# Three projected query tiles between the attention's first scores, and an opening that scales tokens from PSUM

## The chip, the cores and the metric

The kernel runs on 1 core of one Trainium2 chip (trn2). The metric is the device time of one execution in microseconds (us); lower is better.

## The reference

A two-layer encoder trunk is applied to two sequences (`x_prompt` and `x_sample`, 512 tokens of 1,024 numbers each), which share one set of weights. 16 learned meta tokens stand before every sequence and are dropped from the output. All is float32.

- Every layer computes h = h + Mixer(RMSNorm(h)) and then h = h + SwiGLU(RMSNorm(h)).
- Layer 0's mixer is multi-head latent attention (4 heads) beside a short gated convolution; both read one projection of the normalised input, by `mla_w_in`.
- Layer 1's mixer is grouped-query attention: `qkv = h @ w_qkv`, 8 query heads and 2 key/value heads of 128 columns. Queries and keys are RMS-normalised for each head, multiplied by a gain and rotated by two-dimensional positions:

```
q = rms_norm(q, q_g); k = rms_norm(k, k_g)
q = concat(rotate(q[..., :64], ang_rows), rotate(q[..., 64:], ang_cols))   # k likewise
o = softmax(q k^T / sqrt(128)) v
rotate(x1, x2) = (x1 cos - x2 sin, x2 cos + x1 sin)
```

## The kernel before

**Products.** Each float32 operand is held as a high part, rounded to the matmul's format (`_hi`), and the residue (`_lo`). A product is three matmuls, low x high, high x low and high x high (`product`, L164 to L166). The high part is rounded on ScalarE (ACT), the residue is subtracted on VectorE (DVE) or, for weights, on GpSimd (POOL).

**Order of work.** There is no planner. Each engine's instructions are written out by hand as a loop; the phases pass hooks to one another (`then`, `vector_at`, `gpsimd_at`, `items_at`), and engines wait for semaphore counts. Each engine and each DMA queue works its list strictly in order.

**Opening (`gates_steps`).** Eight token tiles of 128 x 1,024 (`x_rows`) and weight units of 128 x 1,024 are loaded by SyncE (SP), meta tokens and small gains by ScalarE's queue. For each tile TensorE transposes 8 blocks into two PSUM banks (`turn_tile`, L485), ScalarE copies them to `h` (`copy_tile`, L368), VectorE multiplies `h` by the norm's gain into `xg` (`scale_tile`, L565), ScalarE rounds (`round_tile`, L374), VectorE subtracts (`split_tile`, L571). ScalarE also rounds the weight units (`round_unit`, L361), GpSimd splits them (L462), and ScalarE squares the rows for the norm (L380). `group(q)` multiplies one weight unit with 352 token columns, 24 matmuls; 36 groups follow one another. The first needs 3 tiles and meta (`ready_for`). Transposition of all 49 rows of gains (L524) waits for all seven small DMAs. TensorE's order is: tile 0, gains, meta, tiles 1 to 5, group 0, tiles 6 and 7, groups 1 to 4, the first scale rows, group 5.

**Layer 1's projections (`qkv_steps`).** `work` has 25 tiles of 128 tokens x 512 columns: 9 of keys and values, then 8 and 8 of queries; numbers 17 to 24 are the last 8 (heads 4 to 7). A tile is 24 matmuls of 512 columns on TensorE, then on ScalarE four squares with a row sum and one copy (`L1267`, `L1273`), on GpSimd a multiplication by the gain (L1288), on VectorE the rotation (`rotate`, `rope_heads`, L661 to L666: six operations on 128 x 256). The last tile is rotated by GpSimd within the attention (`rotate_last`, L1382 to L1390, at tiles 3, 4 and 6). `invert_last` finds the inverse norms of the last 8 tiles on VectorE in five parts, at tiles 3 to 7.

```
banks = [n % 6 for n in range(ends[1])] + [6, 7, 0, 1, 2, 3, 6, 7]     # L1173
if 3 <= n < 8: invert_last(dve, link, n - 3)                            # L1407
if n in (3, 4, 6): rotate_last(pool, (3, 4, 6).index(n))                # L1411
```

**Layer 1's attention (`attention_steps`).** 16 units (sequence, head) of 4 query tiles make 64 tiles n; the keys are new in every fourth unit. For tile n: TensorE makes the scores (two halves, three matmuls each; banks 0 to 3 in turn), VectorE the row maximum (`maximum`, L2072), ScalarE the exponentials (L1898), VectorE the reciprocal of their sum (`invert`, L2079), GpSimd the normalisation and a repeat of the meta columns (L1831, L1835), TensorE transposes the probabilities (`turn_probs`, L1993, L1999, from step n + 2), ScalarE rounds them (L1874), VectorE subtracts (L2049), TensorE multiplies with the values (`output`). GpSimd stages the queries and keys of the unit after next (L1796, L1769) at the second to fourth tile of a unit; TensorE transposes them (L1961). VectorE's step n is: reciprocal of tile n - 1, maximum of n, hook `vector_at`, the finished output's residue, staged items, residues of tile n - 2.

Of the kernel before, what the change touches and what calls it, by code (L numbers as in the profile page):

```python
# [93 lines left out]
def program(nc, x_prompt, x_sample, meta_tokens, mix_norm_g, ffn_norm_g, mla_w_in, mla_q_a_g, mla_kv_a_g,  # L94
# [3 lines left out]
    with ctx:  # L98
# [153 lines left out]
        def gates_steps():  # L252
# [7 lines left out]
            const_in, gains_in, x_in = sem("const_in"), sem("gains_in"), [sem(f"x_in{i}") for i in range(9)]  # L260
            made, turned, gains_t, gains_ready = sem("made"), sem("turned"), sem("gains_t"), sem("gains_ready")
# [37 lines left out]

            def seqs(a, lo, hi):  # L300
                return a.rearrange("p (s t) -> p s t", s=SEQS)[:, :, lo:hi]
# [7 lines left out]
            def sync(sp, load_piece):  # L309
# [38 lines left out]
            def scalar(act, round_piece):  # L348
                act.dma_start(meta_rows, meta_tokens).then_inc(x_in[8], 16)
                for n, (src, l) in enumerate(((mix_norm_g, 0), (ffn_norm_g, 0), (mix_norm_g, 1), (ffn_norm_g, 1))):  # L350
                    act.dma_start(g_rows[KC * n:KC * (n + 1), :],
                                  src[l].rearrange("(c p) -> c p", p=P)).then_inc(gains_in, 16)
# [10 lines left out]
                def copy_tile(i):  # L363

                    act.wait_ge(turned, place(i))
                    t0 = tile_column(i)
                    b = 4 + 2 * (i % 2)
                    A.activation(h[:, :, t0:t0 + P], PS[:, b:b + 2, :].rearrange("p b (c t) -> p (b c) t", c=4),  # L368
                                 ACT.Copy).then_inc(h_copied, 1)
# [12 lines left out]
                def copy_meta():  # L382
                    act.wait_ge(turned, 2)
                    for s in range(SEQS):
                        last = A.activation(h[:, :, s * LEN:s * LEN + META],
                                            PS[:, 3, 0:KC * META].rearrange("p (c t) -> p c t", c=KC), ACT.Copy)
# [92 lines left out]
            def tensor(pe):  # L479
# [23 lines left out]
                def group(q):  # L503
# [10 lines left out]
                    if n < START:  # L514
                        pe.wait_ge(x_split, ready_for[g])
                    for k in range(KC):
# [6 lines left out]
                pe.wait_ge(gains_in, 16 * 7)  # L523
                T.transpose(PS[:, 2, 0:49], g_rows, ident[0:49, 0:49]).then_inc(gains_t, 1)  # L524
# [18 lines left out]
            def vector(dve):  # L543
# [15 lines left out]
                def scale_tile(i):  # L559

                    dve.wait_ge(h_copied, place(i))
                    t0 = tile_column(i)
# [27 lines left out]
                def drain(q):  # L590
# [8 lines left out]
                V.tensor_copy(gain_cols[:, :], PS[:, 2, 0:49]).then_inc(gains_ready, 1)  # L599
                dve.wait_ge(gains_ready, 1)  # L600
                scale_tile(0)
                dve.wait_ge(h_copied, 2)
                V.tensor_tensor(meta_xg, h[:, :, 0:META], gain.unsqueeze(2).broadcast_to([P, KC, META]),
                                ALU.mult).then_inc(x_scaled, 1)
                split_tile(0)
                scale_tile(1)
# [5 lines left out]
                for i in range(2, 8):  # L612
                    scale_tile(i)
                    split_tile(i - 1)
                find_rstd(0)
                split_tile(7)
# [537 lines left out]
        def qkv_steps():  # L1154
# [18 lines left out]
            banks = [n % 6 for n in range(ends[1])] + [6, 7, 0, 1, 2, 3, 6, 7]  # L1173
# [53 lines left out]
            def sync(sp):  # L1227
# [8 lines left out]
                at = work[last][1] % TILES * P  # L1236
# [1682 lines left out]
```

## Time and profile before

| What | us |
|---|---|
| median of 3 runs (lowest to highest) | 2351.49 (2349.76 to 2353.48) |
| the profiled execution, its own time | 2351.51 |
| its span (first to last instruction) | 2349.7 |
| TensorE busy | 2286.0 |
| VectorE, GpSimd, ScalarE busy | 1254.6, 1245.1, 900.0 |

The profile is of one execution. "Span" runs from the first instruction to the last. PE is TensorE's matmuls, PEld its weight loads, DVE VectorE, ACT ScalarE, POOL GpSimd, SP SyncE; a q behind a name is an engine's DMA queue. L12 is line 12 of the kernel. A matmul's duration overlaps that of the next, so the distance of starts is its price; so it is with VectorE's and ScalarE's operations, to a lesser degree. "Idle before" is the time in which the engine had nothing to run before an instruction, with what ended it. PEclk is the granted clock of TensorE as a share of its full 2.4 GHz.

### The profile page before, as it was taken

The numbers are of one execution on the slowest core, as the hardware profiler recorded it, in microseconds if no ns is written. First come the engines' busy times: TensorE is split into PE (matmuls) and PEld (weight loads), VectorE is DVE, ScalarE is ACT, GpSimd is POOL, SyncE is SP. The second block draws the span as 40 slices with busy tenths as digits, with TensorE's granted clock in tenths as the row PEclk, the third lists the DMA queues.
The fourth block names the chain that finished last, engine by engine and source line by source line (L and its number), as shares of the span: only waits on it lengthen the run. The fifth ranks groups of instructions, "written<-read, shape, count | busy, mean of one in ns | idle before, by whom it ended". The sixth has DMA issues, their size and how long they took to land.

```text
span 2349.7 us, 37598 instructions
## 1 busy us (share of the span) xinstructions
PE 2286.0 (97%) x14574; PEld 2084.4 (89%) x14574; DVE 1254.6 (53%) x2017; ACT 900.0 (38%) x1893; POOL 1245.1 (53%) x1048
## 2 busy tenths in 40 slices
PE   7999989999999999999999998999999999999998
PEld 7999878999999999999998778988878888888887
DVE  5221467459444444444449568855954444444444
ACT  5125666445222222222225446754532222222222
POOL 1344388545455555555543347764555555555561
PEclk9999999999999999999999999999999999999999
DMA  5131001432111111111112000023211111111112
GB/s 207 46 107 64 23 20 41 161 86 72 50 50 46 55 55 55 50 50 46 43 48 76 28 3 2 2 84 92 72 54 53 51 54 52 49 53 51 54 54 76
DMA packets 187505, 137.26 MB, mean 58 GB/s; under 512 B 7361, under 2 KB 176210, under 8 KB 187330
## 3 DMA queue, kind: packets, MB, share of 16 engines
q1 hardware_dynamic: 187200, 134.77, 18.7%
q8 instruction: 118, 1.93, 0.3%
q14 instruction: 57, 0.47, 0.1%
q10 hardware_dynamic: 130, 0.09, 0.0%
HBM read 121.69 MB, written 12.85 MB: 57 GB/s over the span
## 4 chain that ended last, share of the span: by engine, by line
PE 81%; DVE 10%; issue 4%; ACT 3%; POOL 2%; DMA 0%; ACTq 0%; DVEq 0%; POOLq 0%
PE PS L164 26%; PE PS L166 26%; PE PS L165 26%; PE PS L1993 1%; DVE stat L2072 1%; DVE w_lo L2049 1%; DVE b_lo L2693 1%; PE PS L1961 1%; DVE x_raw L2689 1%; DVE x_hi L2720 0%; DVE x_lo L216 0%; DVE t L2713 0%; POOL w_lo L462 0%; ACT w_hi L1874 0%; DVE t L2711 0%
## 5 line engine op out<-in xcount | busy, mean ns | idle before, releaser
L2387 POOL TENSOR_TENSOR w_lo<-stage,w_hi 128x512 fp32r<-128x512 f32 x374 | 506.4, 1358 | 613.7 <-ACT w_hi L2383 611.5
L2383 ACT ACTIVATE w_hi<-stage 128x512 fp32r<-128x512 f32 x374 | 233.2, 628 | 558.5 <-PE PS L166 558.4
L2786 DVE TENSOR_TENSOR hT<-hT,PS 128x528 f32<-128x528 f32 (+1 forms) x384 | 266.6, 695 | 309.4 <-PE PS L166 308.7
L164 PE MATMUL PS<-x_hi,w_lo 128*128 128x264 f32 (+2 forms) x1092 | 352.8, 323 | 8.2 <-DVE x_lo L571 5.1
L164 PE MATMUL PS<-s_hi,w_lo 128*128 128x264 f32 (+1 forms) x1104 | 354.4, 321 | 4.1 <-DVE s_lo L2732 3.1
L166 PE MATMUL PS<-s_hi,w_hi 128*128 128x264 f32 (+1 forms) x1104 | 353.9, 321 | 0.0
L165 PE MATMUL PS<-s_lo,w_hi 128*128 128x264 f32 (+1 forms) x1104 | 352.6, 319 | 0.0
L166 PE MATMUL PS<-x_hi,w_hi 128*128 128x264 f32 (+2 forms) x1092 | 351.7, 322 | 0.0
L165 PE MATMUL PS<-x_lo,w_hi 128*128 128x264 f32 (+2 forms) x1092 | 351.1, 322 | 0.0
L164 PE MATMUL PS<-b_hi,w_lo 128*128 128x264 f32 (+1 forms) x864 | 278.4, 322 | 1.4 <-DVE a L2796 1.4
L165 PE MATMUL PS<-b_lo,w_hi 128*128 128x264 f32 (+1 forms) x864 | 277.5, 321 | 0.0
L166 PE MATMUL PS<-b_hi,w_hi 128*128 128x264 f32 (+1 forms) x864 | 276.8, 320 | 0.0
L164 PEld LDWEIGHTS PS<-x_hi,w_lo 128*128 128x128 f32 x1092 | 206.4, 189 | 20.8 <-issue 5.3
L164 PEld LDWEIGHTS PS<-s_hi,w_lo 128*128 128x128 f32 x1104 | 207.6, 188 | 19.4 <-issue 4.8
L166 PEld LDWEIGHTS PS<-s_hi,w_hi 128*128 128x128 f32 x1104 | 207.8, 188 | 15.9
L165 PEld LDWEIGHTS PS<-s_lo,w_hi 128*128 128x128 f32 x1104 | 207.3, 188 | 16.3
L166 PEld LDWEIGHTS PS<-x_hi,w_hi 128*128 128x128 f32 x1092 | 206.6, 189 | 11.6
L165 PEld LDWEIGHTS PS<-x_lo,w_hi 128*128 128x128 f32 x1092 | 206.1, 189 | 11.8
L164 PEld LDWEIGHTS PS<-b_hi,w_lo 128*128 128x128 f32 x864 | 162.5, 188 | 16.9 <-issue 4.5
L166 PEld LDWEIGHTS PS<-b_hi,w_hi 128*128 128x128 f32 x864 | 162.6, 188 | 12.6
L165 PEld LDWEIGHTS PS<-b_lo,w_hi 128*128 128x128 f32 x864 | 162.5, 188 | 12.2
L164 PE MATMUL PS<-x_lo,w_lo 128*128 128x264 f32 (+1 forms) x480 | 154.1, 321 | 3.4 <-issue 2.1
(373 smaller groups left out, 4917.5 us busy)
## 6 DMA issues: line engine op xcount, KB each, us to landing
stage<-in_ffn_w SPq DMA_DIRECT2D x280, 256.0 KB, 2.8
stage<-in_even_w_out SPq DMA_DIRECT2D x32, 256.0 KB, 2.7
stage<-in_odd_w_out SPq DMA_DIRECT2D x32, 256.0 KB, 2.7
stage<-in_mla_w_in SPq DMA_DIRECT2D x12, 512.0 KB, 6.5
stage<-in_gqa_w_qkv SPq DMA_DIRECT2D x12, 512.0 KB, 3.7
h_spill<-hT SPq DMA_DIRECT2D x8, 528.0 KB, 5.1
hT<-h_spill SPq DMA_DIRECT2D x8, 528.0 KB, 6.7
conv_hi<-s_hi SPq DMA_DIRECT2D x4, 528.0 KB, 2.7
```

The lines of the kernel that those rows point to most:

```text
L164: T.matmul(out, a_lo, b_hi, start=first, stop=False)
L165: T.matmul(out, a_hi, b_lo, start=False, stop=False)
L166: return T.matmul(out, a_hi, b_hi, start=False, stop=last)
L1961: last = T.transpose(PS[:, bank, j * P:(j + 1) * P], k_stage[:, staged_main(s, j), c * P:(c + 1) * P] if kind == "k" else q_stage[:, stage ...
L1993: T.transpose(PS[:, 4 + turn[("p", n, 0)] % 2, c * P:c * P + m], p[0:m, c * P:(c + 1) * P], ident[0:m, 0:m])
L2049: V.tensor_tensor(lo, src, hi.bitcast(F32), ALU.subtract).then_inc(lo_ready, 1)
L2072: V.tensor_reduce(shifts[0:rows, b:b + 1], PS[0:rows, 2 * (n % 2):2 * (n % 2) + 2, 0:HALF], mybir.AxisListType.XY, ALU.min).then_inc(shift, 1)
L2383: A.activation(ring(w_hi, n), source(n), ACT.Copy).then_inc(rounded, 1)
L2387: G.tensor_tensor(ring(w_lo, n), source(n), ring(w_hi, n).bitcast(F32), ALU.subtract).then_inc(split, 1)
L2689: V.tensor_tensor(x_of(c, s), x_of(c, s), tt_row, ALU.mult).then_inc(xhat, 1)
L2693: V.tensor_tensor(bl(c // 4, s, c % 4), x_of(c, s), bh(c // 4, s, c % 4).bitcast(F32), ALU.subtract).then_inc(x_split, 1)
L2786: V.tensor_tensor(o, o, sums(st.slot), ALU.add).then_inc(drained, 1)
```

## The change

Two parts.

**Opening.** VectorE scales tokens from the transposition's PSUM banks instead of `h`; it no longer waits for ScalarE's copy, and the copy now waits for the scaling. Gains are transposed and copied in two goes, the first norm's 8 columns first, with a semaphore of their own; all 49 rows again after tile 1. SyncE loads the first weight unit before tile 2 (before: after it); ScalarE's queue issues the first gain before meta. ScalarE starts with rounding the first unit and then, for each tile, rounds before it copies. TensorE multiplies group 0 after tile 3, group 1 after tile 5.

**Layer 1.** Only 22 tiles are projected before the attention; tile 22 is multiplied after scores 1, tiles 23 and 24 after scores 2 (`tensor_at`), evicted by ScalarE at steps 1, 2 and 3 (`scalar_at`). The last four tiles (21 to 24) are scaled by GpSimd at tiles 8, 12, 16 and 20 and rotated by VectorE in three parts each, at tiles 12 to 14, 16 to 18, 20 to 22 and 24 to 26, with tables loaded anew. `invert_last` moves to tiles 5 to 9. Exponentials of tile 2 are put before the rounding of staged items.

```diff
-                for i in range(3):
+                for i in range(2):
                     load_x(i)
                 load_unit(0)
-                load_x(3)
+                for i in range(2, 4):
+                    load_x(i)
...
                 def copy_tile(i):
-                    act.wait_ge(turned, place(i))
+                    act.wait_ge(x_scaled, place(i))
...
+                round_unit(0)
+                round_tile(0)
+                round_meta()
                 copy_tile(0)
                 copy_meta()
-                round_tile(0)
+                round_tile(1)
                 copy_tile(1)
-                round_meta()
                 for i in range(2, 8):
+                    round_tile(i)
                     copy_tile(i)
-                    round_tile(i - 1)
-                    if i in (2, 3, 4):
-                        round_unit(i - 2)
-                    if i == 4:
+                    if i in (2, 3):
+                        round_unit(i - 1)
+                    if i == 3:
                         square_meta(0)
-                    if i >= 4:
-                        square_rows(i - 4)
-                round_tile(7)
+                    if 3 <= i < 7:
+                        square_rows(i - 3)
...
-                for i in range(1, 6):
+                turn_tile(1)
+                pe.wait_ge(gains_in, 16 * 6)
+                pe.wait_ge(gains_ready, 1)
+                T.transpose(PS[:, 2, 0:49], g_rows, ident[0:49, 0:49]).then_inc(gains_t, 1)
+                for i in range(2, 4):
                     turn_tile(i)
                 group(0)
+                for i in range(4, 6):
+                    turn_tile(i)
+                group(1)
                 for i in (6, 7):
                     turn_tile(i)
-                for q in range(1, 5):
+                for q in range(2, 5):
                     group(q)
...
-                    dve.wait_ge(h_copied, place(i))
+                    dve.wait_ge(turned, place(i))
                     if i >= 2:
                         dve.wait_ge(x_split, place(i - 2))
-                    V.tensor_tensor(xg[i % 2], h[:, :, t0:t0 + P], gain.unsqueeze(2).broadcast_to([P, KC, P]),
+                    V.tensor_tensor(xg[i % 2], turned_tile(i), gain.unsqueeze(2).broadcast_to([P, KC, P]),
...
+                scale_tile(2)
+                split_tile(1)
+                split_tile(2)
+                dve.wait_ge(gains_t, 2)
+                V.tensor_copy(gain_cols[:, KC:49], PS[:, 2, KC:49]).then_inc(gains_ready, 1)
+                scale_tile(3)
+                for i in range(4, 8):
                     scale_tile(i)
                     split_tile(i - 1)
...
-            banks = [n % 6 for n in range(ends[1])] + [6, 7, 0, 1, 2, 3, 6, 7]
+            roped_late, filling = len(work) - 4, len(work) - 3
+            banks = [n % 6 for n in range(ends[1])] + [6, 7, 2, 3, 6, 7, 6, 7]
...
+            def sync_late(sp):
+                sp.wait_ge(last_roped, 1)
+                load_late_table(sp, last)
...
             def vector_at(dve, link, n):
-                if 3 <= n < 8:
-                    invert_last(dve, link, n - 3)
+                if 5 <= n < 10:
+                    invert_last(dve, link, n - 5)
+                unit, j = divmod(n - 12, MAIN)
+                if 0 <= unit < 4 and j < 3:
+                    rotate_late(dve, roped_late + unit, j)
 
             def gpsimd_at(pool, n):
-                if n in (3, 4, 6):
-                    rotate_last(pool, (3, 4, 6).index(n))
+                if n in (8, 12, 16, 20):
+                    scale_tile(pool, roped_late + n // 4 - 2)
+
+            def tensor_at(pe, n):
+                if n == 0:
+                    multiply(pe, filling)
+                if n == 1:
+                    multiply(pe, filling + 1)
+                    multiply(pe, filling + 2)
+
+            def scalar_at(act, n):
+                if n in (1, 2, 3):
+                    evict(act, filling + n - 1)
...
             def wait_scores(pe, n):
                 if n == 0:
-                    pe.wait_ge(copied, len(work) - 2)
+                    pe.wait_ge(copied, ends[1])
+                if n == 1:
+                    pe.wait_ge(copied, roped_late)
...
-                    if not L0 and n == first_steps.queries_after + 5:
+                    if not L0 and n == first_steps.queries_after + 3:
                         stage_heads(1)
...
+                            if not L0:
+                                first_steps.wait_weights(act)
                             round_values(0)
```

`rotate_late` makes the same six operations on VectorE as `rotate_last` made on GpSimd, two for each part: two products, two products, a difference and a sum; both inputs of each lie in SBUF. `multiply` and `evict` are the bodies of the former loops. `wait_weights` waits for the last projected tile, since the values' high part overwrites the weights. The probabilities' first transposition waits for the eviction of tile 23, the first output for that of tile 24.

## Rows read from the trace of the kernel before

**Rows 1.** the page, busy time of each engine: us (share of the span), instructions.

```profile
PE 2286.0 (97%) x14574; PEld 2084.4 (89%) x14574; DVE 1254.6 (53%) x2017; ACT 900.0 (38%) x1893; POOL 1245.1 (53%) x1048
```

**Rows 2.** timeline, opening, TensorE: start, us, engine, line, what, [idle before <- released by].

```profile
5.48 1.94 PE L485 MATMUL PS<-ident,wide 128*128 128x128 f32 x8 [5.48 <-DMA wide<-in_x_prompt]
...
23.38 0.63 PE L164 MATMUL PS<-x_hi,w_lo 128*128 128x352 f32 x1 [5.13 <-DVE x_lo L571]
...
29.23 1.91 PE L485 MATMUL PS<-ident,wide 128*128 128x128 f32 x16
```

**Rows 3.** timeline, opening: ScalarE, VectorE and GpSimd.

```profile
8.89 1.23 DVE L565 TENSOR_TENSOR mid<-hT,gain_cols 128x1024 f32<-128x1024 f32 x1
...
14.14 1.05 ACT L374 ACTIVATE x_hi<-mid 128x1024 fp32r<-128x1024 f32 x1
...
16.22 2.65 POOL L462 TENSOR_TENSOR w_lo<-stage,w_hi 128x1024 fp32r<-128x1024 f32 x1 [14.65 <-ACT w_hi L361]
...
17.08 2.87 DVE L565 TENSOR_TENSOR mid<-hT,gain_cols 128x1024 f32<-128x1024 f32 x1 [0.44 <-ACT hT L368]
...
19.87 3.37 DVE L571 TENSOR_TENSOR x_lo<-mid,x_hi 128x1024 fp32r<-128x1024 f32 x1
```

**Rows 4.** timelines, end of layer 1's projections and start of its attention: ScalarE, TensorE.

```profile
1383.97 0.37 ACT L1267 ACTIVATE wide<-PS,stat 128x128 f32<-128x128 f32 x1 [3.93 <-PE PS L166]
...
1400.67 0.37 ACT L1267 ACTIVATE wide<-PS,stat 128x128 f32<-128x128 f32 x1 [1.82 <-PE PS L166]
...
1403.63 0.39 PE L164 MATMUL PS<-s_hi,s_lo 128*128 128x264 f32 x1 [1.52 <-ACT tmp L1898]
...
1405.30 0.66 PE L1993 MATMUL PS<-ident,tmp 128*128 128x128 f32 x4 [0.23 <-POOL tmp L1831]
...
1419.81 0.63 PE L1993 MATMUL PS<-ident,rope 128*128 128x128 f32 x4 [1.25 <-DVE s_lo L2049]
```

**Rows 5.** timeline, layer 1's attention, TensorE, the same place of two neighbouring units.

```profile
1445.26 0.65 PE L1993 MATMUL PS<-ident,tmp 128*128 128x128 f32 x4 [0.22 <-POOL tmp L1831]
...
1454.34 0.66 PE L1993 MATMUL PS<-ident,gain_rows 128*128 128x128 f32 x4 [0.20 <-POOL gain_rows L1831]
```

**Rows 6.** windows, a unit and one with new keys: PE, PEld, DVE, ACT, POOL.

```profile
1453.01:1462.09 9.08, 8.88 (x76) 8.67 (x75) 7.89 (x16) 6.83 (x17) 6.53 (x10) 1.00 0.01 2
1433.93:1445.03 11.10, 9.84 (x79) 8.97 (x77) 8.54 (x19) 7.60 (x20) 6.58 (x11) 1.00 0.00 0
```

**Rows 7.** sources, opening: weight load issued at 2.1, third token tile at 1.7.

```profile
DMA to landing us min/median/max: 7.1/7.1/7.1
...
DMA to landing us min/median/max: 6.2/6.2/6.2
```

**Rows 8.** windows, opening: busy of five engines, granted clock, DMA share, GB/s.

```profile
23.00:24.00 1.00, 0.62 (x2) 0.65 (x3) 0.90 (x2) 0.97 (x2) 1.00 (x1) 0.50 0.42 70
```

**Rows 9.** timeline, opening, VectorE: the drain of a later group.

```profile
61.25 0.52 DVE L594 TENSOR_TENSOR wide<-PS,mid 128x352 f32<-128x352 f32 x1 [3.34 <-PE PS L166]
```

**Rows 10.** timeline, layer 1's attention, VectorE: reciprocal of one tile, maximum of the next.

```profile
1453.01 0.16 DVE L2079 RECIPROCAL stat<-stat 128x1 f32<-128x1 f32 x1
1453.20 0.71 DVE L2072 TENSOR_REDUCE stat<-PS 128x1 f32<-128x528 f32 x1
```

**Rows 11.** timeline, layer 1's attention, GpSimd: normalisation and repeat of a tile.

```profile
1455.25 1.04 POOL L1831 TENSOR_TENSOR rope<-rope,stat 128x512 f32<-128x512 f32 x1
1456.25 0.35 POOL L1835 TENSOR_TENSOR tmp<-rope,stat 128x96 f32<-128x96 f32 x1
```

**Rows 12.** timelines, VectorE and GpSimd: two-operand operations in SBUF side by side.

```profile
1324.82 2.60 DVE L661 TENSOR_TENSOR tmp<-wide,rope 128x256 f32<-128x256 f32 x1 [3.35 <-POOL wide L1288]
...
1324.73 2.40 POOL L1225 TENSOR_TENSOR w_lo<-stage,w_hi 128x1024 fp32r<-128x1024 f32 x1
...
1414.60 0.97 DVE L188 SCALAR_TENSOR_TENSOR stat<-stat,tmp 128x32 f32<-128x32 f32 x1
```

**Rows 13.** groups by form, 1420 to 1560: count | busy, mean ns | idle.

```profile
L2049 DVE TENSOR_TENSOR w_lo<-PS,w_hi 128x512 fp32r<-128x512 f32 x59 | 40.6, 688 | 12.0 <-ACT w_hi L1874 11.9
```

More of the change, by code:

```diff
@@ L1283, in gpsimd @@
                 pool.wait_ge(consts, 48)
-                for n, (b, i) in enumerate(work):
-                    heads = heads_of(n)
-                    pool.wait_ge(copied, n + 1)
-                    o = place(n).rearrange("p (h n) -> p h n", h=heads)
-                    G.tensor_tensor(o, o, gains[b == 2].unsqueeze(1).broadcast_to([P, heads, HD]),
-                                    ALU.mult).then_inc(scaled, 1)
+                for n in range(roped_late):
+                    scale_tile(pool, n)
                     if n in piece_after:
@@ L1292, in gpsimd, with multiply @@
                     then(n)
+            def multiply(pe, n):
+                b, i = work[n]
+                t0 = token_column(i)
+                block_ = sum(n >= e for e in ends)
+                earlier = [m for m in range(n) if banks[m] == banks[n]]
+                if earlier:
+                    pe.wait_ge(copied, earlier[-1] + 1)
+                else:
+                    steps.wait_bank(pe, banks[n])
+                if banks[n] == 7 and not earlier:
+                    pe.wait_ge(norm.rstd_ready, 2)
+                if i == MAIN:
+                    pe.wait_ge(gathered, 2)
+                for k in range(KC):
+                    if n == 0 or n in ends:
+                        pe.wait_ge(split, 4 * block_ + k // 2 + 1)
+                    if n < ONCE:
+                        norm.wait_x(pe, 1 - i // TILES, k)
+                    out = PS[0:meta_cols, banks[n], :] if i == MAIN else PS[:, banks[n], :]
+                    hi, lo = (metas[part][:, k, :] if i == MAIN else (x_hi, x_lo)[part][:, k, t0:t0 + P] for part in range(2))
+                    product_ = product(out, hi, lo,
+                                       weights(block_, 0, k), weights(block_, 1, k), k == 0, k == KC - 1)
+                product_.then_inc(done, 1)
             def tensor(pe, then):
-                for n, (b, i) in enumerate(work):
-                    t0 = token_column(i)
+                for n in range(filling):
                     if n == 1:
@@ L1300, in tensor @@
                         norm.average(pe, 1)
-                    block_ = sum(n >= e for e in ends)
-                    earlier = [m for m in range(n) if banks[m] == banks[n]]
-                    if earlier:
-                        pe.wait_ge(copied, earlier[-1] + 1)
-                    else:
-                        steps.wait_bank(pe, banks[n])
-                    if banks[n] == 7 and not earlier:
-                        pe.wait_ge(norm.rstd_ready, 2)
-                    if i == MAIN:
-                        pe.wait_ge(gathered, 2)
-                    for k in range(KC):
-                        if n == 0 or n in ends:
-                            pe.wait_ge(split, 4 * block_ + k // 2 + 1)
-                        if n < ONCE:
-                            norm.wait_x(pe, 1 - i // TILES, k)
-                        out = PS[0:meta_cols, banks[n], :] if i == MAIN else PS[:, banks[n], :]
-                        hi, lo = (metas[part][:, k, :] if i == MAIN else (x_hi, x_lo)[part][:, k, t0:t0 + P] for part in range(2))
-                        product_ = product(out, hi, lo,
-                                           weights(block_, 0, k), weights(block_, 1, k), k == 0, k == KC - 1)
-                    product_.then_inc(done, 1)
+                    multiply(pe, n)
                     if n == MAIN - 1:
@@ L1358, in vector @@
                 dve.wait_ge(consts, 48)
-                for n in range(last):
+                for n in range(roped_late):
                     if n == 3:
```

149 lines of the change are left out of this document (95 added, 54 removed).

## The prediction

> **What bounds the kernel now.** I read the page's busy line first: TensorE is busy 97% of the span [rows 1]. A change that adds or drops no matmul can therefore only fill TensorE's idle time or make new idle time, and I looked for idle time where the diff has its hands: the opening and the start of layer 1's attention.
>
> Opening, TensorE's timeline: it stands 5.48 us for the first tokens and, later, 5.13 us before the first projection at 23.38, released by the vector engine's residue of x [rows 2]. The engines behind that wait: one token tile costs the scalar engine a rounding of 1.05 us and a copy of about as much, and the vector engine a scaling of 1.23 and a residue of as much; but the scaling at 17.08 took 2.87 and the residue at 19.87 took 3.37. Both overlap GpSimd's split of the first weight unit, 16.22 to 18.87, and the next ones [rows 3]. 17.08 + 2.87 = 19.95 is one plain scaling after 18.87: the vector operation stood until GpSimd's ended.
>
> Layer 1's attention, by timelines and windows. A projected query tile takes TensorE (1400.67 - 1383.97)/3 = 5.57 us, by the scalar engine's evictions of tiles 21 and 24; the next scores wait 1.52 for the exponentials, the first transposition of probabilities follows at 1405.30, and later the tiles still stumble, as at 1419.81 for 1.25 us [rows 4]. Once in step, a unit (a head, four tiles) takes 1454.34 - 1445.26 = 9.08 us and TensorE waits 0.20 in it, on GpSimd's normalisation [rows 5]. So there TensorE is the bound by a hair. The vector engine is busy 7.89 of 9.08 us, and 8.54 of 11.10 in the unit where new keys are prepared [rows 6]: it has 1.19 and 2.56 us to give. That is what the vector rotations of the change have to fit into.
>
> **The change, part by part.**
>
> *Opening.* First unit of weights before the third token tile in SyncE's queue: before, it was issued at about 2.1 and landed 7.1 later, the third tile at 1.7 and 6.2 [rows 7]. They swap: weights at about 7.9, tile at 9.3. ScalarE now stands at its queue's head for those weights with the rounding and copying of all tiles behind it; rounding ends at 9.0, which costs nothing, because the first scaled tile exists only then: transposition to 7.42 [rows 2], gains, scaling of 1.23 = 9.3. The gains' own DMA goes first in ScalarE's queue and the tokens of meta one place later; both land before 7.42 and cost nothing. GpSimd splits unit 0 from 9.1 to 11.8 (2.65). Scaling now reads PSUM, so only residues can collide: tile 0 until 13.0, meta 13.5; tile 2 is transposed after the copy of tile 0, by about 13.6, scaled by 14.9, residues of tiles 1 and 2 end at 16.1 and 17.3. So group 0 starts at about 17.4 in place of 23.38: 6.0 earlier. Given back: tiles 4 and 5 are transposed behind it (16 transpositions took 1.91 [rows 2], so 2.0) and the last tile waits for ScalarE's copy of tile 5, which three squares and a unit are queued before, some 1.7 which is an estimate from those durations. On the other side, TensorE's granted clock was 0.50 at the first group [rows 8], that is 1.2 GHz, after 5 us without work: group 0 took 23.38 to 29.23 = 5.85 [rows 2] where a later one takes 3.34 + 0.52 = 3.86 by the vector engine's drains [rows 9], so 2.0 were lost. Its waits are now under 2 us each; it may stay at 2.4 GHz, and even if it doesn't, a slow group 0 uses up the wait for tile 5. I count 1.5. Sum -6.0 + 2.0 + 1.7 - 1.5 = **-3.8**; ends -1.5 (the residues collide again, the clock falls) and -5.5 (no wait for tile 5). The second copy of gains, a short one, and group 2's wait for it lie beside this and cost nothing. From there to the attention TensorE hardly waits, so the gain lasts.
>
> *Filling.* Tiles 22 to 24 go behind scores 1 and 2. Start at 1383.9: one score and the next head's transpositions take 1405.30 - 0.23 - 1403.63 = 1.44, two more scores some 0.8 each, three tiles 16.7: first probabilities transposed at 1403.6, against 1405.30 [rows 4]: -1.7. The eviction of tile 24 now sits on ScalarE before exponentials 4, values are rounded only after all weights are used, with GpSimd's split of values and the queries of head 2 queued behind; both were as late before. The inversion of norms, five pieces on VectorE whose operations stand up to 0.97 us [rows 12], moves from tiles 3 to 7 to tiles 5 to 9, where VectorE gives 1.19/4 = 0.3 a tile: what it delays there it delayed before. GpSimd loses the last rotation. Taken: **-1.5**; ends 0 (the pieces stop a pipeline already in step) and -4 (most of the stumbling goes).
>
> *Rotations in units 3 to 6.* Four tiles, each as three pairs of two-operand operations on VectorE, behind the maximum of tiles 0, 1 and 2 of a unit. In the projections, where the first three of them ran, VectorE had idle time and they cost nothing; the fourth was GpSimd's. A pair alone costs two operations of 0.29 or a little more (below), 0.7. But look where it lands: a reciprocal at 1453.01, the maximum at 1453.20 [rows 10], and that same reciprocal releases GpSimd's normalisation, 1.04 us, then its repeat, 0.35 [rows 11]. When the maximum ends, some 0.7 after the reciprocal, the normalisation runs until 1.3 after it. And rows show what a rotation does then: L661 beside GpSimd's split of 2.40 us took 2.60, that is until 0.29 after GpSimd's end, its own part; an inversion's operation on 32 columns beside a normalisation took 0.97 [rows 12]. The split that reads one operand from PSUM stays at 688 ns all through [rows 13]. So the first of the pair ends at 1.6, GpSimd's repeat at 1.8, the second at 2.1: 1.4 us, not 0.7. Twelve pairs are 16.8 us; VectorE has 3 x 1.19 + 2.56 = 6.1 to give: **+10.7** on a loop that TensorE does not outrun. Ends: +2.3 (12 x 0.7 less 6.1: no blocking) and +13.8 (half of the idle time is not where it's needed). I take the blocked price since L661 itself is the row.
>
> The rows have no rotation beside a normalisation, both with two operands. The Trainium skill, "SBUF — State Buffer", section "Who interferes with whom", says that a VectorE operation with two SBUF inputs and a GpSimd operation that reads SBUF exclude each other for the whole instruction, and that VectorE with at most one SBUF input doesn't take part. By that rule every rotation queues behind the normalisation as above; without it the sum would take the +2.3. The same rule speaks for the scaling from PSUM.
>
> GpSimd's four scalings of 512 columns, each at most a normalisation and a repeat long, 1.4 [rows 11], move into tiles 8, 12, 16 and 20, where it stages nothing; it is busy 6.53 of 9.08 us [rows 6]; staging of head 1 two tiles earlier, the three tables' DMAs behind the last weights and SyncE's wait for the first late rotation (behind it only the next stage's loads, due far later) lie beside other work: 0. The new bank waits are for evictions a tile old: 0.
>
> Sum: -3.8 - 1.5 + 10.7 = +5.4. The profiled execution is 2351.51 (span 2349.7), the median of the runs 2351.49, so **2356.9**. A measurement of this kernel tells about 0.2%, 4.7 us, from no change; this is just beyond it.
>
> **Rivals.**
> A, the forecast: 2356.9, own range 2353 to 2361. Chance 0.48, of it 0.31 beyond 4.7 us.
> B, rotations hide: they end before the next reciprocal matters, +2.3. It decides if a pair costs under 1.0: then 12 x 1.0 - 6.1 = 5.9 is all but paid by 5.3. For it: three of the four tiles' steps contain idle time; against it: the 2.60 row. -3.8 - 1.5 + 2.3 = -3.0, 2348.5. Chance 0.22, faster in 0.07.
> C, opening gives 1 only, since residues wait for GpSimd and ScalarE's longer queue holds the last tiles: 2351.5 - 1 - 1.5 + 10.7 = 2359.7. Chance 0.12.
> D, clock: with TensorE busy some 9 of 12 us in units 3 to 6 it is granted 1.2 GHz for a stretch as at the opening [rows 8]; 3 us more: 2360. Chance 0.08.
> E, the good side: opening -5.5, filling -4, rotations +2.3: 2344.3, faster. It decides if the stumbling after 1405 came from GpSimd's rotation and not from the inversion. Against it: VectorE's inversions are as long as before. Chance 0.10.
> That the change doesn't do what it says would show as TensorE idle unchanged in both places; too little to have a chance of its own.
>
> Faster 0.10 + 0.07 = 0.17; slower 0.31 + 0.12 + 0.08 = 0.51; same 0.32. The range 2346 to 2364 leaves out part of E and the far end of A with C.
>
> **What would show it.** First projection at 17 to 18 us, tiles 4 and 5 transposed behind it; drain of group 4 four us earlier. First transposition of probabilities 1.8 us closer to the eviction of tile 21, no wait for exponentials before it. In units 3 to 6: rotations of 0.6 to 0.9 us beside normalisations, units of 11 to 12 us in place of 9.08, TensorE waiting on GpSimd's normalisation and on residues for over 2 us each. Wrong if those units keep 9.1 to 9.8 us, or if the first group starts later than 20.

## The result and the profile after

| | median us (runs) | ratio to before, 95% interval |
|---|---|---|
| before, beside it | 2350.81 (6) | |
| changed kernel | 2359.49, 2356.69 to 2362.46 (6) | 1.0036 [1.0025, 1.0046] |
| changed kernel, second time (below) | 2358.39, 2355.31 to 2361.18 (7) | 1.0031 [1.0020, 1.0043] |

The change makes the kernel 8.7 us slower, and both intervals lie above 1. The forecast was 2356.9, slower, in a range of 2346 to 2364.

The page of the changed kernel, busy time, to set beside [rows 1]:

```profile
span 2358.2 us, 37608 instructions
PE 2291.5 (97%) x14575; PEld 2087.0 (89%) x14575; DVE 1258.2 (53%) x2024; ACT 899.7 (38%) x1893; POOL 1242.4 (53%) x1042
```

The span is 8.5 us longer, and the shares tell nothing. The answer is in two short stretches.

**Opening.** TensorE's waits up to the first projection, beside [rows 2]:

```profile
4.75 1.94 PE L493 MATMUL PS<-ident,wide 128*128 128x128 f32 x8 [4.75 <-DMA wide<-in_x_prompt]
11.60 1.94 PE L493 MATMUL PS<-ident,wide 128*128 128x128 f32 x8 [1.39 <-ACT hT L376]
13.79 1.94 PE L493 MATMUL PS<-ident,wide 128*128 128x128 f32 x8 [0.25 <-ACT hT L376]
17.29 0.40 PE L164 MATMUL PS<-x_hi,w_lo 128*128 128x352 f32 x1 [1.56 <-DVE x_lo L587]
```

The wait of 5.13 is gone, and group 0 starts at 17.29 in place of 23.38. VectorE and GpSimd at the same time, beside [rows 3]:

```profile
11.12 1.60 DVE L587 TENSOR_TENSOR x_lo<-mid,x_hi 128x1024 fp32r<-128x1024 f32 x1
17.17 1.22 DVE L581 TENSOR_TENSOR mid<-PS,gain_cols 128x1024 f32<-128x1024 f32 x1
...
17.82 2.41 POOL L470 TENSOR_TENSOR w_lo<-stage,w_hi 128x1024 fp32r<-128x1024 f32 x1 [6.19 <-ACT w_hi L370]
```

The scaling that reads PSUM takes 1.22 us although a split of GpSimd begins in the middle of it; before, it took 2.87 in that company.

**Units 3 to 6 of layer 1's attention.** One unit, from the reciprocal of tile 20 to that of tile 24, as a window (PE, PEld, DVE, ACT, POOL, PEclk), and then two waits of TensorE in it from its timeline, to set beside [rows 6] and [rows 5]:

```profile
1459.05:1470.94 11.89, 9.51 (x74) 8.68 (x74) 11.20 (x24) 6.81 (x16) 8.68 (x11) 1.00 0.01 2
```

```profile
1461.83 0.63 PE L2076 MATMUL PS<-ident,rope 128*128 128x128 f32 x4 [0.45 <-DVE w_lo L2136]
1464.96 0.63 PE L2076 MATMUL PS<-ident,tmp 128*128 128x128 f32 x4 [1.31 <-DVE s_lo L2136]
```

The unit takes 11.89 us where it took 9.08, and VectorE is busy 11.20 of it: the bound has moved from TensorE to VectorE. VectorE and GpSimd for one tile of that kind (start, us, engine, line):

```profile
1455.87 0.16 DVE L2166 RECIPROCAL stat<-stat 128x1 f32<-128x1 f32 x1
1456.07 0.71 DVE L2159 TENSOR_REDUCE stat<-PS 128x1 f32<-128x528 f32 x1
1456.69 0.74 DVE L1428 TENSOR_TENSOR stage<-wide,stage 128x256 f32<-128x256 f32 x1
1457.36 0.56 DVE L1429 TENSOR_TENSOR stage<-wide,stage 128x256 f32<-128x256 f32 x1
1457.85 0.68 DVE L2150 TENSOR_TENSOR x_lo<-PS,x_hi 128x512 fp32r<-128x512 f32 x1
...
1456.12 1.04 POOL L1903 TENSOR_TENSOR gain_rows<-gain_rows,stat 128x512 f32<-128x512 f32 x1 [0.52 <-DVE stat L2166]
1457.12 0.53 POOL L1907 TENSOR_TENSOR tmp<-gain_rows,stat 128x96 f32<-128x96 f32 x1
```

Read the ends: the normalisation ends at 1456.12 + 1.04 = 1457.16 and the first rotation at 1457.43, 0.27 later; the repeat ends at 1457.65 and the second rotation at 1457.92, again 0.27 later. Each rotation stands until GpSimd's operation is over and then does its own 0.27 us. From the end of the maximum to the next split the pair takes 1.16 us here, 1.29 in the second tile of a unit. TensorE's waits in the unit add up to 2.4 us, 2.2 of them for VectorE's residues and 0.2 for GpSimd; before they were 0.2 in all.

**Where the 8.5 us are.** To follow one execution against another I take the start of each tile's reciprocal (VectorE, L2079 before, L2166 after), subtract that of the profiled execution of before, and subtract the shift that had built up by the first eviction of layer 1's projections, so that what happened earlier drops out. In the changed kernel that shift is -5.1; behind it tile 7 stands at -1.2, tile 11 at +1.7 (by then both kernels have filled and inverted everything), tile 27 and all later ones at +13.6. -5.1 + 13.6 = +8.5.

### The profile page after: what moved, and what is told of

It reads as the page before. It is cut to its first block, busy times and chain, and to the rows that moved or that the text cites. A ratio compares the mean times of both kernels' runs of the same rounds, so it can differ in the third digit from the quotient of the medians.

```text
span 2358.2 us, 37608 instructions
## 1 busy us (share of the span) xinstructions
PE 2291.5 (97%) x14575; PEld 2087.0 (89%) x14575; DVE 1258.2 (53%) x2024; ACT 899.7 (38%) x1893; POOL 1242.4 (53%) x1042
## 4 chain that ended last, share of the span: by engine, by line
PE 81%; DVE 10%; issue 4%; ACT 3%; POOL 2%; DMA 0%; DVEq 0%; SPq 0%; ACTq 0%; POOLq 0%
PE PS L164 26%; PE PS L166 26%; PE PS L165 26%; PE PS L2076 1%; DVE stat L2159 1%; DVE w_lo L2136 1%; DVE b_lo L2780 1%; PE PS L2044 1%; DVE x_raw L2776 1%; DVE x_hi L2807 0%; DVE x_lo L216 0%; DVE t L2800 0%; POOL w_lo L470 0%; DVE t L2798 0%; DVE t L2802 0%
## 5 line engine op out<-in xcount | busy, mean ns | idle before, releaser
L164 PEld LDWEIGHTS PS<-b_hi,w_lo 128*128 128x128 f32 x864 | 162.5, 188 | 16.8 <-issue 4.4
```

Of the source, the lines that this page charges most:

```text
L164: T.matmul(out, a_lo, b_hi, start=first, stop=False)
```

## The experiments

All kernels below are edits of the changed one unless a heading says otherwise; all times stand beside runs of before on the same chip. Differences from before: before took 2350.7 in the first four, 2350.6 in the next four, 2352.1 in the next three and 2351.3 in the last.

**1 and 2. The two parts alone.** The edit: only the hunks of the opening, or only those of layer 1, put into the kernel before.

> The kernel before with the changed opening alone. If the two parts of the change are worth what the trace of the changed kernel shows where they stand (the eviction of projected tile 21 starts 5.06 us earlier, copy_rows 5.36 earlier, the waits of the layer 0 projections 5.55 earlier), the span is 5.1 to 5.5 us shorter than before: about 2345.5 us. Rival: the projections give some of the gain back once nothing behind them is moved, as the forecast's case of an opening worth 1 us said: 2349 to 2350 us.

> The kernel before with the changed layer 1 part alone, with the old opening. Theory: filling and inversion lose 1.7 us together, the rotations 11.8, so 13.5 us over before: 2364.3 us. Rival: the two parts are not independent (the 5 us of the opening move the layer 1 part against nothing, but the split of the tails is late only when head 1's staging meets it): then 2361 or less, or 2367 or more.

Measured: opening alone 2347.91, ratio 0.9983 [0.9975, 0.9992]; layer 1 alone 2364.10, ratio 1.0057 [1.0043, 1.0070]. By the tiles' reciprocals the layer 1 part costs 13.4 in the one and 13.6 in the changed kernel: the parts are independent. The opening gives 4.6 us by the two spans (2349.7 to 2345.1), as expected, but only 2.8 by the medians, between the expectation and its rival; number 10 looks into this. The layer 1 part came out as expected.

**3. No rotation.**

```diff
-                    V.tensor_tensor(t[0], x1, cos, ALU.mult)
-                    V.tensor_tensor(t[1], x2, sin, ALU.mult)
                 if part == 1:
-                    V.tensor_tensor(t[2], x2, cos, ALU.mult)
-                    V.tensor_tensor(t[3], x1, sin, ALU.mult).then_inc(last_products, 1)
+                    V.engine_nop().then_inc(last_products, 1)
```

(and the two operations of part 2 likewise.)

> The changed kernel without the arithmetic of the four late tiles' rotation (24 operations of VectorE left out, so four query tiles of layer 1 go unrotated into the attention; every wait and signal stays, and so do the scaling on GpSimd, the table loads and the inversion). Theory: the 11.8 us that the tiles from 10 to 27 lose are VectorE's time in units 3 to 6, so nearly all of it comes back: 2347 to 2349 us. Rival: GpSimd's scaling of the late tiles (1.45 us each, four of them) and its slower repeats (0.53 for 0.35 us) hold the units up, and the rotations only fill waits: 4 us or less comes back, 2355 us or more.

This kernel leaves the rotation out and so computes something else; it only prices those operations. Measured: 2347.64, that is 3.1 under before. The tile curve ends at +2.4 in place of +13.6: the 24 operations cost 11.1 us, as the theory had it. Of the 2.4, 1.7 are there at tile 11, and 0.7 come at tile 19, where GpSimd's scaling of 1.28 us stands between two normalisations and TensorE waits 0.55 for the second. A unit of this kernel as a window:

```profile
1455.82:1464.91 9.09, 8.87 (x76) 8.65 (x76) 7.92 (x18) 6.85 (x16) 7.75 (x12) 1.00 0.01 2
```

Without them it is the unit of before again, TensorE 8.87 of 9.09 us.

**4. The pair at the end of VectorE's step**, behind the splits of the tile instead of behind the maximum.

```diff
+            def vector_end(dve, n):
                 unit, j = divmod(n - 12, MAIN)
                 if 0 <= unit < 4 and j < 3:
                     rotate_late(dve, roped_late + unit, j)
```

> The changed kernel with each pair of rotation operations issued at the end of VectorE's step, behind the splits of that tile, in place of behind the maximum. Blocking theory (the pair is dear because it meets GpSimd's normalisation on the SBUF): at the end of the step the normalisation is over or nearly, the first operation of a pair falls from 0.74 to 1.20 us to about 0.56, and 12 pairs give back 2 to 5 us: 2354 to 2357 us. Plain throughput theory (the unit is as long as VectorE's work in it, wherever the pair stands): within 1 us of the changed kernel, 2358 to 2360 us. Third way: the pair now delays the next tile's reciprocal, on which GpSimd waits, and the time rises by up to 3 us.

Measured: 2354.99, 4.2 over before where the changed kernel is 8.7 and 7.8 over. VectorE in the rotation of two tiles, and GpSimd:

```profile
1451.87 0.43 DVE L1428 TENSOR_TENSOR stage<-wide,stage 128x256 f32<-128x256 f32 x1
1452.22 0.41 DVE L1429 TENSOR_TENSOR stage<-wide,stage 128x256 f32<-128x256 f32 x1
1452.56 0.15 DVE L2169 RECIPROCAL stat<-stat 128x1 f32<-128x1 f32 x1
...
1440.08 1.50 DVE L1429 TENSOR_TENSOR stage<-wide,stage 128x256 f32<-128x256 f32 x1
...
1439.84 1.47 POOL L1882 TENSOR_TENSOR w_lo<-mid,w_hi 128x512 fp32r<-128x512 f32 x1
```

Alone, the pair takes 0.69 us, from 1451.87 to 1452.56. Beside GpSimd's split of values one operation takes 1.50 and ends 1441.58 - 1441.31 = 0.27 after it. The blocking theory holds. The end of the step isn't free of GpSimd either: six of the twelve pairs still stood a while behind a split, a scaling or a staging, and together the twelve took 10.5 us of VectorE's time (14.8 in the changed kernel; 12 x 0.69 would be 8.3). From tile 11 to the end the curve rises by 8.6 us (-0.5 to +8.1), against 11.8 in the changed kernel. Both rises include the 0.7 us that number 3 shows at tile 19 without any rotation, if it recurs here. So some eight tenths of what VectorE spends is paid, in both places, although VectorE had idle time in every unit of before. The rest of the gain over the changed kernel's trace, 2.2 us, comes from elsewhere: the clock. Windows of about tiles 4 to 8 in this kernel, then in the changed one, whose code is the same there (PE, PEld, DVE, ACT, POOL, PEclk):

```profile
1405.00:1410.00 5.00, 4.53 (x40) 4.35 (x39) 4.80 (x11) 2.77 (x8) 2.31 (x5) 1.00 0.00 0
1410.00:1415.00 5.00, 4.06 (x34) 3.61 (x33) 4.74 (x11) 3.42 (x8) 3.51 (x6) 1.00 0.01 2
```

```profile
1405.00:1410.00 5.00, 4.05 (x19) 4.05 (x20) 4.36 (x9) 3.25 (x9) 3.49 (x6) 0.51 0.01 3
1410.00:1415.00 5.00, 5.00 (x37) 5.00 (x37) 3.26 (x8) 2.02 (x6) 1.64 (x3) 0.81 0.00 0
```

At 0.51 TensorE is at 1.2 GHz, and 19 matmuls go through where 40 did. Tile 7 stands at -1.2 in the trace with the low clock and at -3.4 in the other.

**5. One operation at a time.** The same 24 operations singly at the step's end, spread over tiles 12 to 40.

```diff
+                for k in range(24):
+                    if n == 12 + k * 30 // 24:
+                        rotate_late(dve, roped_late + k // 6, k % 6 // 2, k % 2)
```

> As the kernel with the rotation at the step's end, but the same 24 operations issued one at a time, in place of in pairs, over tiles 12 to 40 (four in five tiles get one) instead of over three tiles of each of the units 3 to 6. Slack theory: in the units of four tiles VectorE works 7.89 of 9.08 us, so it has 1.19 us a unit to give; 3.2 operations of 0.34 us a unit are 1.1 us and find room, where three pairs a unit (2.1 us) did not. The 8.6 us that the rotations cost in that kernel fall to 1 or 2: 2347 to 2349 us, about 7 us under it. Rival, serial theory: each operation delays the next tile's reciprocal by its own length, whatever idle time there is elsewhere, so 24 operations cost 24 times 0.34, 8 us, wherever they stand: 2354 to 2356 us.

Measured: 2351.95, between the two (1.3 over before). The curve rises from -0.4 to +5.7, 6.2 us or 0.26 for each operation, where the 24 took 9.0 us of VectorE's time (0.34 each where nothing held them). The slack theory falls: 1.19 us of idle time a unit took up about a third of what was put there. Serial is nearer, and I read the reason in what follows an operation at the step's end: the next tile's reciprocal, which releases GpSimd, which releases TensorE's transposition.

**6. The inversion at the step's end too** (tiles 5 to 9), on top of 4.

> As the kernel with the rotation at the step's end, and the five pieces of the inversion (tiles 5 to 9) moved there too. The reading so far: with the tensor clock whole the tiles 7 to 9 lose 2.9 us to the inversion, because VectorE is full there (4.8 of 5 us), so the place within the step hardly matters: 2354 to 2356 us, within 1 us of that kernel. Rival: the pieces are dear because they hold back the split of that tile's probabilities, on which TensorE waits: 1.5 to 3 us less, 2352 to 2353.5 us.

Measured: 2353.93; 1.1 under number 4 by the medians, which lies between the two ranges, and 2.0 by the curve: tile 11 stands at -2.5 in place of -0.5. The curve speaks for the rival, that the place matters. The last operation of the inversion behind the maximum, with what GpSimd did there (changed kernel), and at the step's end:

```profile
1422.57 1.21 DVE L189 SCALAR_TENSOR_TENSOR rn_all<-stat,rn_all 128x32 f32<-128x32 f32 x1
...
1422.44 1.29 POOL L1320 TENSOR_TENSOR wide<-wide,gain_rows 128x512 f32<-128x512 f32 x1
```

```profile
1422.40 0.19 DVE L189 SCALAR_TENSOR_TENSOR rn_all<-stat,rn_all 128x32 f32<-128x32 f32 x1
```

It stood until the scaling of a late tile ended (1423.73) and ended 0.05 later. That scaling, at tile 8, is new in the change: in the kernel before the same operation took 0.66. All twelve operations of the inversion together take 6.5 us in the changed kernel (6.0 before) and 2.6 at the step's end, where eleven of them take 0.17 to 0.19.

**7. The changed kernel again.**

> The changed kernel again. In its first trace the granted clock is 0.51 and 0.81 from 1405 to 1415 us of the span, in the trace of the kernel with the rotation at the step's end, whose code is the same up to tile 12, it is 1.00 there. Chance theory: the dip belongs to the execution and not to the program, and costs 2.2 us when it comes; this trace may show either, and the runs of one kernel spread by some 6 us. Rival: the dip belongs to this program and is there again. Either way the median is 2358 to 2361 us, 8 to 9.5 us over before.

Measured: 2358.39, and the trace has no low clock in tiles 4 to 8 but has one in tiles 12 to 14:

```profile
1405.00:1415.00 10.00, 8.10 (x64) 7.26 (x62) 9.57 (x21) 5.51 (x13) 5.18 (x8) 1.00 0.00 1
1430.00:1435.00 5.00, 5.00 (x24) 4.59 (x23) 3.24 (x8) 0.67 (x2) 1.59 (x3) 0.50 0.04 13
```

The median is as expected, though 7.8 over before where I had 8 to 9.5. The low stretch belongs to the execution, not to the program. Of the nine traces with the filling four have it in tiles 4 to 8 (tile 7 at -1.1 to -1.2; without it at -3.3 to -3.9); of the five without filling one has a mild one there. Whether the filling makes it likelier can't be told from so few.

**8. Opening alone with the old inversion at the step's end.**

> The changed opening with the layer 1 part of before, and the five pieces of the inversion (tiles 3 to 7) at the end of VectorE's step instead of behind the maximum. If the place doesn't matter: as the opening alone, 2347 to 2349 us. Rival: it takes 1.5 to 3 us off that.

Measured: 2348.60, ratio 0.9987 [0.9978, 0.9996]: no better than the opening alone. Moving the pieces pays in number 6, where the tiles are in step; in tiles 3 to 7 it doesn't. But there the step's end is no free place: five of the twelve operations still took 0.54 to 0.66 us and all of them 4.8 together (2.6 in number 6), so this run doesn't tell whether they would be cheap to move. Its trace has a granted clock of 0.73 from 1405 to 1410 us and stands 0.4 us later for it.

**9. The spread rotation on GpSimd** in place of VectorE, behind the repeat of its tile.

> As the spread rotation, tiles 12 to 40, one operation at a time, but on GpSimd behind the repeat of its tile instead of on VectorE. In the kernel before, GpSimd's rotation operations of the last tile took 0.73 us each. Theory: GpSimd works 6.53 of 9.08 us a unit and waits for the reciprocal behind most tiles, so 3.2 operations (2.2 us) fit into its 2.5 us, and the 6.2 us that the spread rotation costs on VectorE fall to 1 to 3: about 2347 to 2349 us. Rival: a GpSimd operation behind the repeat holds back the next tile's normalisation where GpSimd does not wait, and stages and scalings come on top: 6 us or more, 2352 us or more.

Measured: 2352.27, 0.1 over before. The curve from tile 11 rises by 5.0 us (VectorE: 6.2), between my two cases. The operation on GpSimd here, and on VectorE in number 5 (duration in ns: least, median, most):

```profile
L1430 POOL TENSOR_TENSOR stage<-wide,stage x16: 718/736/774, 1435.2 to 1501.7; 128x256 f32<-128x256 f32 x16
```

```profile
L1430 DVE TENSOR_TENSOR stage<-wide,stage x16: 415/424/666, 1433.6 to 1502.4; 128x256 f32<-128x256 f32 x16
```

GpSimd has 2.5 us idle a unit; 0.21 of each 0.7 us is paid. I read it so that its waits are for the reciprocal and not all behind the tile at hand; no run tests this by itself.

**10 and 11. Why the opening's gain varies.** In the changed opening TensorE stands 1.4 and 1.56 us before group 0. Number 10 fills both with transpositions that nobody reads; 11 is the opening alone once more.

```diff
+                keep_busy(5)
                 for i in range(2, 4):
                     turn_tile(i)
+                keep_busy(6)
                 group(0)
```

> The changed opening alone, with 5 idle transpositions of the identity into an unused PSUM bank ahead of the turning of tile 2 and 6 ahead of projection group 0, where TensorE waits 1.4 and 1.56 us. In the eight traces with the changed opening so far, group 0's products stand 0.16 us apart from the start in three, and 0.29 us apart for the first 10 to 20 of 24 in five, which costs 1.3 to 2.7 us. Theory: the tensor clock falls because of what TensorE does in the waits ahead of group 0, and with the waits filled all 24 products run at 0.16 us: median 1 to 2 us under the opening alone. Rival: the slow products come whatever TensorE did in these 3 us, and the time is that of the opening alone or up to 1 us over it, for the transpositions delay the turning of tiles 2 and 3 a little.

> The changed opening alone again, beside the kernel whose waits are filled: median 2347 to 2349 us, ratio to before 0.998 to 0.999; its group 0 may run at either spacing.

Group 0 of number 10, with the turning before it, then of number 6, whose opening is the changed one:

```profile
13.76 1.07 PE L493 MATMUL PS<-ident,wide 128*128 128x128 f32 x8 [0.42 <-ACT hT L376]
17.09 0.40 PE L164 MATMUL PS<-x_hi,w_lo 128*128 128x352 f32 x1 [1.61 <-DVE x_lo L593]
```

```profile
17.49 0.63 PE L164 MATMUL PS<-x_hi,w_lo 128*128 128x352 f32 x1 [1.57 <-DVE x_lo L587]
17.92 0.49 PE L165 MATMUL PS<-x_lo,w_hi 128*128 128x352 f32 x1
18.22 0.49 PE L166 MATMUL PS<-x_hi,w_hi 128*128 128x352 f32 x1
```

Eight transpositions took 1.94 us in the opening of the changed kernel and 1.07 after the filled wait, and group 0 then ran at full pace. But the median, 2346.83, is no better than number 11's 2346.44 (ratio 0.9979 [0.9971, 0.9988]); one trace at full pace proves little, since four of eleven unfilled openings had that too. The time is what the rival said: nothing gained. Number 11 itself came out just under its range of 2347 to 2349. Over the traces, the number of group 0's 24 products that stand 0.29 us apart instead of 0.16 was 13 and 19 in the two with the old opening, and 0, 0, 0, 0, 10, 10, 10, 13, 18, 19 and 20 in the eleven with the changed one unfilled. Each slow product costs 0.13 us: 0 to 2.6 us, and with it the shift of the drain at 61.25 [rows 9] runs from -2.4 to -5.9, -4.2 in the mean of the eleven. Such differences can be part of why 11 runs of one kernel gave -2.8 once and -5.7 the other time; but 1.4 of these 2.9 us lie in the runs of before beside them (2350.7 and 2352.1), and only 1.5 in the kernel. Whether the waits decide the pace stays open.

**12. Rotations in VectorE's waits.** On top of 6, 24 single operations, one ahead of every split of a transposed tail, the rest at every third step's end.

```diff
                     if lag <= n < len(tiles) + lag and closes_group(n - lag):
+                        if not L0:
+                            first_steps.vector_gap(dve, n)
                         split_bank(("ptail", n - lag, 0))
```

> The changed kernel with the inversion at the step's end (tiles 5 to 9) and VectorE's 24 rotation operations one at a time in other places: from tile 12 on, one right ahead of the split of a transposed tail, where VectorE waits 0.25 to 0.53 us for ScalarE's rounding (every second tile), and the rest, one at the end of every third step. Gap theory: an operation costs nothing where VectorE already waits for ScalarE, and 0.26 us at the step's end, so some 14 operations are free and 10 cost 2.6 us; with filling and inversion at -2.5 us the layer 1 part is worth about 0, and the time is that of the opening alone or up to 1.5 us more: 2347 to 2349 us. Rival, serial theory: each costs 0.26 us wherever it stands in the step, 6.2 us in all: 2351 to 2352 us.

Measured: 2352.23, 0.9 over before; the curve rises from -2.5 to +5.4, 7.9 us, where the gap theory had 2.6 and number 5 shows 6.2. The gap theory falls:

```profile
1441.91 1.31 DVE L1435 TENSOR_TENSOR wide<-stage 128x256 f32<-128x256 f32 x1
1443.23 0.42 DVE L2151 TENSOR_TENSOR w_lo<-PS,w_lo 32x256 fp32r<-32x256 f32 x1
...
1441.91 1.03 POOL L1918 TENSOR_TENSOR gain_rows<-gain_rows,stat 128x512 f32<-128x512 f32 x1
```

GpSimd works while VectorE waits there, so the operation stood until 1442.94 and took 1.31 in a gap of 0.5. The 24 operations took 15.7 us in all; the waits did pay for half of that, but being held cost as much again.

**A version that beats both.** The opening alone: 2347.91 and 2346.44 in two sittings of 11 runs, ratios 0.9983 [0.9975, 0.9992] and 0.9979 [0.9971, 0.9988]. No variant of the layer 1 part got clearly under it; even number 3, which leaves out the dearest item, the rotation, is only even with it (2347.64 beside 2347.91).

The curve of each kernel, in us against before:

| | median | tile 7 | tile 11 | tile 50 |
|---|---|---|---|---|
| changed | 2359.49 | -1.2 (low clock) | +1.7 | +13.6 |
| changed, again | 2358.39 | -3.4 | -0.5 | +12.4 |
| 3, no rotation | 2347.64 | -1.2 (low clock) | +1.7 | +2.4 |
| 4, step's end | 2354.99 | -3.4 | -0.5 | +8.1 |
| 5, spread | 2351.95 | -3.3 | -0.4 | +5.7 |
| 6, inversion too | 2353.93 | -3.9 | -2.5 | +6.1 |
| 9, on GpSimd | 2352.27 | -1.1 (low clock) | +1.8 | +6.8 |
| 12, in gaps | 2352.23 | -3.9 | -2.5 | +5.4 |

## Why the prediction held, and which of its terms did not

**What bounds the kernel** was read rightly: TensorE by a hair in the units of four tiles, and a kernel whose VectorE work per unit then exceeds TensorE's. The sum was +5.4; measured are +8.7 by the medians and +8.5 in the profiled execution. That adds up from -5.1 for the opening, +1.7 up to tile 11 (-0.5 and a low clock of 2.2) and +11.8 behind it, so the terms missed both ways and in part cancelled.

**Opening, -3.8: mis-sized, mechanism right.** Group 0 starts at 17.29 against 17.4 worked out; the scaling from PSUM isn't held (1.22), the residues are (1.60). Tile 5's copy was waited for 0.7 us, not 1.7. The profiled execution gained 5.1 to 5.5, the far end; over eleven traces 4.2. The term for the clock, "I count 1.5", is the one that chance decides, between 0 and 2.6.

**Filling, -1.5: first half right, the step that failed is "what it delays there it delayed before".** The first transposition of probabilities came 1.2 us closer to tile 21's eviction (1.7 worked out), and by tile 7 the gain was 3.4. Then 2.9 of it went by tile 11, the tiles of the inversion, and -0.5 was left. Behind the maximum most of its operations stand until GpSimd's is over, and they now do so in tiles that are in step; that they were cheap before because those tiles waited anyway is argued and not tested by itself. Number 6 moved them, and tile 11 stood 2.0 better. No run leaves out the scaling at tile 8, which falls into the same tiles; it held the last operation for 1.21 us. What staging head 1 earlier costs was set at 0; the earlier staging held the first two rotation operations of tile 20 to 0.82 and 0.83 us (the others took 0.41), a tail's split was queued behind them, and the first scores waited 0.82 for it. That is inside the 1.2.

**The clock, not in the sum: +2.2.** Rival D had it in units 3 to 6 and at 3 us. It came in tiles 4 to 8 of the profiled execution, in tiles 12 to 14 of the next (1.1 us there), and in neither in others.

**Rotations, +10.7 against 11.1 (11.8 with the wait at tile 19): right by two errors that cancel.** I priced a pair at 1.4 us and let 6.1 us of idle time pay for part of 16.8. The pairs took 1.16 to 1.29 us, one 1.6, together 14.8; and idle time paid 3.7, not 6.1. That the figure came out so close is luck. Idle time measured over a unit isn't idle time on VectorE's loop: at the step's end, 10.5 us of VectorE's time cost 8.6 in number 4 and 9.0 cost 6.2 in number 5, each with up to 0.7 for the scaling. The lower end, +2.3 "no blocking", subtracted the same idle time, and was far too low: with most of the blocking gone the rotations still cost 5.5 to 8.6. Rival B with it: at 0.88 a pair in the mean its condition, under 1.0, was met in number 4, and the time still rose.

The price itself came from the row where a two-operand operation stood beside GpSimd's [rows 12], and this was the right row. The rule of the Trainium skill, "SBUF — State Buffer", section "Who interferes with whom", which excludes the two for the whole instruction, agrees with every end read above: 0.27 or 0.28 us after GpSimd's end, four times; and its other half, that an operation with one SBUF input takes no part, agrees with the scalings of 1.22. One thing goes beyond the words I used: the inversion's one-input piece stood as well, 0.88 us on 32 columns until 0.05 after the end of a normalisation, where it takes 0.18 at the step's end. The same section of the Trainium skill makes that exception, for instructions in a mode that uses both ports, and counts `tensor_scalar`, which this piece is, among those that can enter it; in which mode it ran, no row shows.

**Rival C** (the opening gives 1) is ruled out: at the drain of [rows 9] every trace had gained at least 2.4; **rival E** needed rotations at +2.3 and falls with B.

## What to carry to other kernels

Idle time per unit says what an engine could take at most, not what it will: of an operation put into this serial loop (reciprocal, normalisation, transposition, split) six to eight tenths of its time were paid, and half where it stood at VectorE's own waits and met GpSimd there. Before moving VectorE work with its operands in SBUF, look at what GpSimd does in that very spot; the same operation took 0.42 us alone and 0.74 to 1.50 beside GpSimd, and what only moves from one place to another isn't free either. And compare executions tile by tile against a common mark: a clock that dips by chance for some 7 us shifts a single trace by more than most of the terms in question.

## What the hardware showed that I had not expected

- The tensor clock's low stretches differ between executions of the same code: 0.51 and 0.81 in tiles 4 to 8 in one, 1.00 there and 0.50 ten tiles later in the other. The runs of one kernel spread by 4 to 11 us, and such stretches are part of it. Another sits between 560 and 620 us; before and number 4:

```profile
560.00:620.00 60.00, 56.56 (x452) 56.20 (x450) 43.72 (x48) 23.36 (x40) 36.37 (x25) 0.97 0.23 67
```

```profile
560.00:620.00 60.00, 56.59 (x464) 56.23 (x464) 41.47 (x47) 22.48 (x39) 36.59 (x25) 1.00 0.18 54
```

  which moves number 4 ahead by 1.5 us. The Trainium skill, "TensorE: Matmul & The Clock Gate", "Part 1: The HAM clock gate", says that the window in which the gate watches TensorE runs freely and isn't reset when a kernel starts; that could explain it, and no run here shows it by itself.
- In the opening the granted clock column reads 1.00 from 18 to 22 us while group 0's products stand 0.29 us apart instead of 0.16. There the spacing of the products is the better witness.
- GpSimd mostly went first: its normalisation took 1.03 to 1.07 us in every company. But what was queued behind a rotation grew: the repeat from 0.35 to 0.53, a staging from 0.62 to 0.80, the scaling of a late tile from 1.29 to 1.45, and in number 4 the split of values from 1.29 to 1.47.
